# Last stage of a decoder step: squares summed on VectorE, subtractions behind the products, and sample attention values with the probabilities as stationary operand

## What is computed

```python
def rmsnorm(x, g):
    xf = x.astype(jnp.float32)
    y = xf * lax.rsqrt(jnp.mean(xf * xf, axis=-1, keepdims=True) + EPS)
    return (y * g.astype(jnp.float32)).astype(x.dtype)
...
    mn = rmsnorm(mem_prompt, norm_mem[l])
    mk = (mn @ w_xk[l]).reshape(bp, N_MEM, X_HEADS, X_HD)
    mv = (mn @ w_xv[l]).reshape(bp, N_MEM, X_HEADS, X_HD)
...
    q = (h @ wq).reshape(b, L, X_HEADS, X_HD)
    s = jnp.einsum('blhd,bmhd->bhlm', q, mem_k).astype(jnp.float32) * (X_HD ** -0.5)
    p = jax.nn.softmax(s, axis=-1).astype(h.dtype)
    o = jnp.einsum('bhlm,bmhd->blhd', p, mem_v).reshape(b, L, X_WIDTH)
    return o @ wo
...
    o = rmsnorm(o, p['dn_norm']) * jax.nn.silu(d_gate.astype(f32).reshape(b, L, DN_HEADS, DN_DV))
    hm = rmsnorm(hm, p['ml_norm']) * jax.nn.sigmoid(l_o.astype(f32).reshape(b, L, ML_HEADS, ML_DV))
    mix = jnp.concatenate([dn_out, ml_out, s5_out], axis=-1).astype(x.dtype)
    x = x + mix @ p['w_out']
```

## Time and profile before

| | us |
|---|---|
| median of 3 runs (lowest, highest) | 1800.17 (1792.58, 1803.59) |
| profiled execution | 1799.6 |
| its span in the trace | 1797.8 |
| TensorE matmuls busy | 1716.0 (95%) |
| VectorE busy | 718.1 (40%) |
| ScalarE busy | 517.9 (29%) |
| GpSimd busy | 481.9 (27%) |

### The profile page before, as it was taken

One profiled execution on the slowest core, in us unless ns is written; L12 is line 12 of the kernel. 1 busy time (PEld: TensorE's weight loads), 2 busy tenths in 40 slices (PEclk: granted clock), 3 DMA queues, 4 the chain that ended last, 5 costly groups with the idle time before them and its releaser, 6 DMA issues.

```text
span 1797.8 us, 35692 instructions
## 1 busy us (share of the span) xinstructions
PE 1716.0 (95%) x15140; PEld 1568.5 (87%) x15140; DVE 718.1 (40%) x1407; ACT 517.9 (29%) x1140; POOL 481.9 (27%) x303
## 2 busy tenths in 40 slices
PE   6999989998999998899989999999999999999997
PEld 3666679998988996599967789999999999999997
DVE  7746576630565637647254351111111111111245
ACT  3443645311333423213253143102310131013211
POOL 1010212332112213603020013333433333334620
PEclk9999999999999979899998799999999999999998
DMA  4110011112232118102050001111111111111202
GB/s 146 43 48 24 24 47 36 37 46 61 47 64 53 31 34 307 39 13 71 19 239 1 1 24 47 48 47 48 47 47 47 47 46 38 44 47 47 82 19 78
DMA packets 53266, 100.46 MB, mean 56 GB/s; under 512 B 7857, under 2 KB 35873, under 8 KB 52881
## 3 DMA queue, kind: packets, MB, share of 16 engines
q1 hardware_dynamic: 52032, 96.25, 17.3%
q0 software_dynamic: 1104, 2.32, 0.5%
HBM read 90.38 MB, written 7.58 MB: 54 GB/s over the span
## 4 chain that ended last, share of the span: by engine, by line
PE 55%; DVE 4%; POOL 2%; ACT 1%; issue 0%; POOLq 0%; DVEq 0%; ACTq 0%
PE ps L2041 13%; PE ps L2042 13%; PE ps L2043 13%; PE ps L1900 3%; PE ps L1906 3%; PE ps L1908 3%; PE ps L1907 3%; PE ps L2024 1%; PE ps L1870 1%; PE ps L1953 1%; PE ps L1879 1%; POOL feat_r L1844 1%; DVE feat L2397 1%; PE ps L1965 0%; POOL regH_r L1846 0%; DVE feat L2290 0%
## 5 line engine op out<-in xcount | busy, mean ns | idle before, releaser
L2041 PE MATMUL ps<-feat_r,rows_r 128*128 128x352 f32 x1392 | 450.9, 324 | 1.8 <-POOL regW_r L1846 0.9
L2043 PE MATMUL ps<-feat_r,regW_r 128*128 128x352 f32 x1080 | 346.6, 321 | 0.0
L2041 PEld LDWEIGHTS ps<-feat_r,rows_r 128*128 128x128 f32 x1392 | 261.8, 188 | 2.7 <-POOL regW_r L1846 1.2
L2042 PE MATMUL ps<-regH_r,rows_r 128*128 128x352 f32 x768 | 246.9, 322 | 0.0
L2043 PEld LDWEIGHTS ps<-feat_r,regW_r 128*128 128x128 f32 x1080 | 202.8, 188 | 0.0
L2042 PE MATMUL ps<-feat_r,rows_r 128*128 128x352 f32 x624 | 200.2, 321 | 0.0
L2235 ACT ACTIVATE feat<-ps 128x352 f32<-128x352 f32 x96 | 44.5, 464 | 474.9 <-PE ps L2043 474.8
L2455 DVE TENSOR_TENSOR feat_r<-feat,feat_r (+1 forms) x96 | 53.0, 553 | 308.8 <-ACT feat_r L2239 308.8
L445 PE MATMUL ps<-regH,regW 128*128 128x352 f32 x528 | 162.6, 464 | 1.4 <-DVE regH L855 1.4
L445 PEld LDWEIGHTS ps<-regH,regW 128*128 128x128 f32 x528 | 99.6, 192 | 56.4 <-issue 4.2
L1826 POOL TENSOR_TENSOR rows_r<-regW,cst 128x1024 fp32r<-128x1024 f32 x39 | 73.9, 1894 | 272.7 <-PE ps L2043 272.7
(11 more groups left out here) (478 smaller groups left out, 3277.0 us busy)
## 6 DMA issues: line engine op xcount, KB each, us to landing
regW<-w_ff_in SPq DMA_DIRECT2D x45, 512.0 KB, 3.4
regW<-w_in_in SPq DMA_DIRECT2D x27, 512.0 KB, 3.5
regA<-xT_in SPq DMA_DIRECT2D x6, 1408.0 KB, 15.6
ext<-w_ff_in SPq DMA_DIRECT2D x15, 512.0 KB, 3.5
regA<-scr SPq DMA_DIRECT2D x48, 96.0 KB, 3.6
yT_out<-regA SPq DMA_DIRECT2D x12, 352.0 KB, 2.4
feat<-cv_in SPq DMA_DIRECT2D x8, 512.0 KB, 15.2
regH<-ck_in SPq DMA_DIRECT2D x8, 512.0 KB, 7.1
```

Of the source, the lines that this page charges most:

```text
L2041: pe.matmul(bank[:, 0:BW], hi, rhs_hi(k, b), start=(k == 0), stop=False)
L2042: pe.matmul(bank[:, 0:BW], hi, rhs_lo(k, b), start=False, stop=False)
L2043: ins = pe.matmul(bank[:, 0:BW], lo, rhs_hi(k, b), start=False, stop=(k == KT - 1))
```

## The change

The squares of memory go to eight tiles of their own (four of them in `rows`, whose use before makes ScalarE wait for `dd_ready`); VectorE adds them up and one matmul sums over features. The root comes after the second mixer square. VectorE multiplies the mixer tiles by their gates before it takes the variances, two of them ahead of the memory reciprocal and four behind the memory scaling. The subtractions of blocks 0 and 1 come after all six products of the block, and the two subtractions of 1056 columns after those of block 0; the first output tile reads the mixed tiles in the matching order.

The sample values are computed the other way round: the probabilities of one sequence, 16 used columns of 32 (one for each head and token, the rest zero), are the stationary operand, and 512 columns of cached values the moving one. Each sequence has 32 rows of a PSUM bank. ScalarE copies the two banks (`valS`), TensorE transposes them by head, and ScalarE copies from the transposes the columns that belong together into `oT`.

```diff
-        probS, probTS = zml[0:64, 8, 0:512], qkv[:, 2, 0:256]
+        probS = zml[0:64, 8, 0:512]
+        probTS = more[:, 0:512].rearrange("p (m b r) -> p m b r", m=2, b=DB)
+        valS = [more[:, 1152 + g * 512:1152 + (g + 1) * 512] for g in range(2)]
-        msq = [acc[:, k * NMEM:(k + 1) * NMEM] for k in range(4)]
+        msq = [(acc if k < 4 else rows[:, 0, :])[:, (k % 4) * NMEM:(k % 4 + 1) * NMEM] for k in range(KT)]
...
-        ORDER = (6, 7, 0, 1, 2, 3, 4, 5)
+        ORDER = (0, 1, 2, 3, 4, 5, 6, 7)
...
             @block.tensor
-                for k in range(KT):
-                    pe.wait_ge(sem("m_sq"), k + 1)
-                    pe.matmul(ps[7][:, 0:NMEM], ones, msq[k % 4], start=(k == 0), stop=(k == KT - 1)).then_inc(sem("m_ps"), 1)
+                pe.wait_ge(sem("m_sum"), KT - 1)
+                pe.matmul(ps[7][:, 0:NMEM], ones, msq[0], start=True, stop=True).then_inc(sem("m_ps"), 1)
...
-                pe.wait_ge(sem("sc_t"), 1)
+                pe.wait_ge(sem("sc_t"), 4)
                 for b in range(DB):
                     pe.wait_ge(sem(f"vc{b}"), 16)
+                    r = 32 * (b % 4)
+                    for m in range(2):
+                        ins = pe.matmul(ps[4 + b // 4][r:r + 32, :], probTS[:, m, b, :], vc[b][:, m * 512:(m + 1) * 512],
+                                        start=(m == 0), stop=(m == 1))
+                    ins.then_inc(sem("v_done"), 1)
+                for n in range(2, 5):
+                    xo(1, n)
+                for g in range(2):
+                    pe.wait_ge(sem("sv_out"), g + 1)
                     for h in range(XH):
-                        for m in range(2):
-                            at_ = ((h % 2) * 2 + m) * 64 + (h // 2) * 32 + b * DS
-                            ins = pe.matmul(ps[4][:, h * 32 + b * DS:h * 32 + (b + 1) * DS],
-                                            vc[b][:, m * 512 + h * XD:m * 512 + (h + 1) * XD], probTS[:, at_:at_ + DS],
-                                            start=(m == 0), stop=(m == 1))
-                    ins.then_inc(sem("v_done"), 1)
-                for n in range(2, KT):
+                        ins = pe.transpose(ps[3 + g][:, h * P:(h + 1) * P], valS[g][:, h * XD:(h + 1) * XD], ident)
+                    ins.then_inc(sem("sv_tp"), 1)
+                for n in range(5, KT):
                     xo(1, n)
-                pe.wait_ge(sem("sc_out"), 1)
+                pe.wait_ge(sem("sc_out"), 2 * XH)
...
             @block.scalar
                 act.wait_ge(sem("mem_in"), 16)
+                act.wait_ge(sem("dd_ready"), 1)
                 for k in range(KT):
-                    if k >= 4:
-                        act.wait_ge(sem("m_ps"), k - 3)
-                    act.activation(msq[k % 4], memv[:, k, :], ACT.Square).then_inc(sem("m_sq"), 1)
+                    act.activation(msq[k], memv[:, k, :], ACT.Square).then_inc(sem("m_sq"), 1)
                 for j in range(6):
                     act.activation(squares[j], mixed[j], ACT.Square).then_inc(sem("mix_sq"), 1)
-                    if j == 0:
-                        act.wait_ge(sem("m_ps"), KT)
-                act.activation(root[:, 0:NMEM], ps[7][:, 0:NMEM], ACT.Sqrt, bias=pcol("eps"), scale=1.0 / D).then_inc(sem("m_root"), 1)
+                    if j == 1:
+                        act.wait_ge(sem("m_ps"), 1)
+                        act.activation(root[:, 0:NMEM], ps[7][:, 0:NMEM], ACT.Sqrt, bias=pcol("eps"), scale=1.0 / D).then_inc(sem("m_root"), 1)
...
                 act.wait_ge(sem("sc_tp"), 1)
-                act.activation(probTS, ps[3][:, 0:256], ACT.Copy).then_inc(sem("sc_t"), 1)
+                act.wait_ge(sem("sv_zero"), 1)
+                for hh in range(2):
+                    for m in range(2):
+                        act.activation(probTS[:, m, :, 0:16].rearrange("p b (g e t) -> p g b e t", g=2, e=2)[:, :, :, hh, :],
+                                       ps[3][:, (hh * 2 + m) * 64:(hh * 2 + m + 1) * 64].rearrange("p (g b t) -> p g b t", g=2, b=DB),
+                                       ACT.Copy).then_inc(sem("sc_t"), 1)
...
                 for n in range(KT):
                     high(0, n)
-                act.wait_ge(sem("v_done"), DB)
-                act.activation(oT[:, :, SEQ:T], ps[4][:, 0:XH * 32].rearrange("p (h t) -> p h t", h=XH), ACT.Copy).then_inc(sem("sc_out"), 1)
-                for n in range(2, KT):
+                for g in range(2):
+                    act.wait_ge(sem("v_done"), 4 * g + 4)
+                    act.activation(valS[g], ps[4 + g][:, :], ACT.Copy).then_inc(sem("sv_out"), 1)
+                for n in range(2, 5):
+                    square(1, 1, n)
+                for g in range(2):
+                    act.wait_ge(sem("sv_tp"), g + 1)
+                    for h in range(XH):
+                        act.activation(oT[:, h, SEQ + 16 * g:SEQ + 16 * g + 16].rearrange("p (b t) -> p b t", t=DS),
+                                       ps[3 + g][:, h * P:(h + 1) * P].rearrange("p (b r) -> p b r", r=32)[:, :, h * DS:(h + 1) * DS],
+                                       ACT.Copy).then_inc(sem("sc_out"), 1)
+                for n in range(5, KT):
                     square(1, 1, n)
...
             @block.vector
+                for k in range(1, KT):
+                    dve.wait_ge(sem("m_sq"), k + 1)
+                    if k > 1:
+                        dve.wait_ge(sem("m_sum"), k - 1)
+                    dve.tensor_tensor(msq[0], msq[0], msq[k], ALU.add).then_inc(sem("m_sum"), 1)
+
+                def gated(j):
+                    dve.wait_ge(sem("mix_sq"), j + 1)
+                    dve.scalar_tensor_tensor(mixed[j], mixed[j], pcol("dn" if j < 3 else "ml"), gates[j], ALU.mult, ALU.mult)\
+                       .then_inc(sem("mix_g"), 1)
+
+                gated(0)
+                gated(1)
                 dve.wait_ge(sem("m_root"), 1)
...
+                for j in range(2, 6):
+                    gated(j)
                 dve.wait_ge(sem("dd_ready"), 1)
                 dve.wait_ge(sem("mix_ss"), 1)
...
-                        if j and b < 2:
-                            mixed_low(b, j - 1)
                     if b < 2:
-                        mixed_low(b, 5)
+                        for j in range(6):
+                            mixed_low(b, j)
+                    if b == 0:
+                        dve.wait_ge(sem("mix_hi"), 2)
+                        for k in range(6, KT):
+                            dve.tensor_tensor(mixed_lo[k], mixed[k], mixed_hi[k], ALU.subtract).then_inc(sem("mix_lo"), 1)
...
+                dve.memset(more[:, 0:512], 0.0).then_inc(sem("sv_zero"), 1)
                 dve.memset(acc[:, 0:1024], 0.0).then_inc(sem("qm_zero"), 1)
```

More of the change, by code:

```diff
@@ L1717, in build @@
         sems.update(zip(again, spare))
-        for n in ("cc_in split_go wo_hi wo_lo mix_hi mix_lo x_hi x_lo mem_in wk_in wv_in m_sq m_ps m_root m_h mix_sq mix_ss mix_v mix_root mix_r mix_g mix_bc mix_done dd_ready "
+        for n in ("cc_in m_sum split_go wo_hi wo_lo mix_hi mix_lo x_hi x_lo mem_in wk_in wv_in m_sq m_ps m_root m_h mix_sq mix_ss mix_v mix_root mix_r mix_g mix_bc mix_done dd_ready "
                   "mk_ps mk_out mv_ps mv_out mem_out gg ge n_sq n_sum n_ps n_root n_h v_step "
-                  "at_s at_max at_exp at_inv at_p at_tp at_t at_o at_out qm_zero qm_ready k_done sc_max sc_exp sc_inv sc_p sc_tp sc_t "
+                  "at_s at_max at_exp at_inv at_p at_tp at_t at_o at_out qm_zero qm_ready k_done sc_max sc_exp sc_inv sc_p sc_tp sc_t sv_zero sv_out sv_tp "
                   "v_done sc_out h_hi h_lo w_hi w_lo relu squared hid_lo f_sq f_sum f_ps f_root f_h y_out".split()):
@@ L2288, in _ @@
                     dve.tensor_scalar(vr[:, blk(b)], vr[:, blk(b)], 1e-34, None, ALU.max).then_inc(sem("mix_v"), 1)
-                for j in range(6):
-                    dve.scalar_tensor_tensor(mixed[j], mixed[j], pcol("dn" if j < 3 else "ml"), gates[j], ALU.mult, ALU.mult)\
-                       .then_inc(sem("mix_g"), 1)
                 for b in range(NB):
@@ L2298, in mixed_low @@
                     dve.tensor_tensor(mixed_lo[j][:, blk(b)], x_, mixed_hi[j][:, blk(b)], ALU.subtract).then_inc(sem("mix_lo"), 1)
-                dve.wait_ge(sem("mix_hi"), 2)
-                for k in range(6, KT):
-                    dve.tensor_tensor(mixed_lo[k], mixed[k], mixed_hi[k], ALU.subtract).then_inc(sem("mix_lo"), 1)
-                dve.wait_ge(sem("mix_g"), 6)
                 for b in range(NB):
```

## The result

The changed kernel took 1771.0 us (median of 4 runs, 1769.2 to 1773.3), the kernel before 1801.1 (4 runs, 1792.6 to 1803.6) beside it on the same chip: a ratio of 0.983, with a 95% interval of 0.980 to 0.986, so 25 to 35 us less. Measured a second time it was 1771.8 (5 runs) against 1801.8, a ratio of 0.985 (0.982 to 0.987). The forecast was 1771.

What follows compares the result with a forecast made beforehand. The prelude was taken as bound by VectorE's chain, with TensorE waiting 7.39 us, and the sample values by TensorE alone. 1799.6 - 9 (prelude) - 20 (sample values) = 1770.6, say 1771 us; range 1762 to 1786.

Steps and rivals of the forecast that it cites:

- moves forward as a whole: After both places: the work is TensorE's and shifts earlier unchanged; the known stop of 2.19 us at 1044.37 stays.
- Start of the prelude: Prelude up to the memory keys: last addition near 690.2, head sums from 691.2, keys at 704.0, 2 us later than before.
- The bound of 704.4: Prelude: latest start given for the memory keys, against 704.0 forecast and 702.1 with no clock loss.
- the clock term: Head sums in the prelude: TensorE meets half clock after idling, costing 2 to 2.5 us.
- First products: Prelude: no wait for VectorE, first L1879 group from 718.8 to 722.7, first value tile 7.06 instead of 8.78.
- The eight subtractions: Prelude, ahead of the second group's products: some 4 us contended by GpSimd plus 1.7 + 3.1, VectorE free near 731.5.
- Rival 2: Prelude: GpSimd and VectorE delay each other over the moved subtractions; prelude gain 5, time 1774.6 us; chance 0.12.
- The values: Sample values: 32 instructions take 5.3 us (two strips abreast 7.1, four 3.5, serial 14.1); the part gains 20 us.
- it gains nothing more: Sample values: if TensorE outruns ScalarE and idles 2 us before the transposes, no further gain, and some clock could be lost.
- Rival 1: Sample values: strips overlap only where program order allows; 11 us, gain 15, time 1775.6 us; chance 0.13.
- Rival 3: Both stretches: narrow matmuls leave TensorE at half clock; output 1.5 late, values 4.5 more late, time 1806 us; chance 0.03.
- The range: Whole kernel: 1762 to 1786 us, from best bounds of 1768 and a worst of 1785 (1799.6 - 3 - 12).

Runs made afterwards that it cites:

- the kernel without a pause: Not identified; the pause before the transposes is gone in two variants of the changed kernel: values on one strip (1780.3 us) and earlier residuals (1772.6 us).

## Why the prediction was right, step by step

Its sum was 9 + 20 = 29 us. The places say 8.0 + 20.8 - 2.2 = 26.6, and the spans 28.3, of which 1.7 lies ahead of the prelude (685.48 against 683.80). The 2.2 is a term that the forecast put at nothing, for the stage between the two places ("moves forward as a whole"). The mechanism was right at both places; that the median falls on the forecast to the microsecond is luck, for the 1.7 and the 2.2 nearly cancel.

*Start of the prelude.* Everything is 1.7 us earlier in the trace, so I add that to the times after. The last addition ended at 689.51 + 1.7 = 691.2, forecast 690.2: the seven follow each other at 0.53 (0.44 and the wait), not at 0.38. TensorE's sum of squares took 1.22, not 0.9. The head sums took 13.18; the forecast had 12.8 (691.2 to 704.0). Keys at 705.6 instead of 704.0. The bound of 704.4 was passed, by the additions and not by the clock; the clock term, 2 to 2.5 in the text though the sum took only 1.9 (704.0 - 691.2 - 10.86), was 13.18 - 10.86 = 2.3.

*First products.* From the keys' start to the first group 14.7 us, forecast 14.8. No wait; TensorE's short idle of 0.69 is the copy. The value tile 7.06, as forecast.

*The eight subtractions.* Mis-sized on the safe side. 2.69 and 2.42 us, where I had some 4 for what was contended and 4.8 for the rest, and VectorE was free at 727.97 + 1.7 = 729.7 instead of 731.5. GpSimd was done with its four tiles at 721.4, before the first subtraction; the tiles took 4.3 us each and not 5.5 to 6. The contention that I looked for there was at the variances instead (1.60, 1.97 and 1.48 for three operations of 0.33; 6.5 for all six, of the 7 allowed), in time that TensorE needs for the keys. Rival 2 is out by the same rows. The second group followed without a wait and ended 0.4 us sooner in its chain than forecast, so of the 1.6 us late at the keys 1.0 was left: output at 745.8 in the time of before, forecast 744.8, a gain of 8.0 instead of 9.

*The values.* 3.68 us where 5.3 was taken, between bounds of 3.5 and 14.1: all four strips side by side. The 1.6 us gained went into the pause of 1.78, as the forecast said of that case ("it gains nothing more"): from the first value matmul to the end of the transposes it had 991.1 - 977.22 = 13.9, and 983.54 - 969.64 = 13.9 was measured. What ends there is the chain of the halves on VectorE and ScalarE, and the run on one strip shows it from the other side: 10.2 us more of matmuls cost 8.2. Clock loss after the pause there was none (the gemms behind it: 12.00 for 40, as 12.10 in the kernel without a pause).

*Rival 1*, strips that overlap only in program order, needed 11 us; 3.68 rules it out. The trace's entry for the line has the 32 starts between 969.6 and 972.7 us, each some 0.59 long:

```profile
L2024 PE MATMUL ps<-feat,more x32: 592/592/617, 969.6 to 972.7; 128*32 128x512 f32 x32
```

The four instructions of one sequence share a strip and take 0.43 each there (13.92 for 32); were the next sequence's to start only after them, 32 starts would spread over 10 us. The Trainium skill, page "TensorE: Matmul & The Clock Gate", Part 3 (packing small matmuls), has matmuls in strict program order at start and end. The measurement differs from it here and decides.

*Rival 3*, narrow matmuls that stay at half clock, had the right stretch but not its length: the head sums began at 0.50 and were at 1.00 from 696, and the values ran at 1.00.

*The range.* Its upper end, 1785, takes 3 us for the prelude, where the working has 5 as the worst; no step gives the 3, and nothing came to hang on it.

## What to carry to other kernels

When a chain of waits sits on one engine while another stands idle, look on that engine for work that nobody needs yet and put it behind the work that is waited for: here reordering alone gave all of the prelude's gain, and moving the squares between engines gave nothing that the times show, since TensorE, idle while the squares were summed elsewhere, had the lower clock behind it. For small matmuls try the wide operand as the moving one, and outputs of 32 rows on different strips: here the first was worth 9.3 to 12.6 us and the second 8.2, and the clock stayed at 1.00 where it had fallen to 0.50. Judge such edits by places inside the kernel as well as by its time, as the time here moved by 10 us with stages that the edit did not touch.

## What had not been expected

Four column strips ran fully abreast, 32 instructions of 512 columns in 3.68 us against 13.92 on one, though the four instructions of a strip stand together in the program. A pause of 8.5 us cost 2.3 us of clock behind it, and filling the middle of it with 3.8 us of matmuls removed that in one trace (10.86) and only part of it in another (12.55), with the same instructions and the same 3.18 us of idle time behind them. Three operations of 64x352 on VectorE, 0.33 each alone, took 1.48 to 1.97 beside GpSimd.
